# A decoder step on one core: the order of bias tables, row sums, gates and loads at its beginning rearranged

## The chip, the cores and the metric

One core of a Trainium2 chip runs the whole kernel. The engines named below are TensorE (PE, with its weight loads as PEld), VectorE (DVE), ScalarE (ACT), GpSimd (POOL) and SyncE (SP). SP and POOL issue nearly all DMAs. The metric is the device time of one execution in microseconds (us), as the median of several runs.

## What is computed

One layer of a decoder for 512 prompt tokens and 8 sample tokens (520 columns in all). The parts that the change touches are the conditioned norm, the projection, the branch gates, the compressed pages and the bias of the three attention branches:

```python
sh1, sc1, gt1, sh2, sc2, gt2 = ada_mod(c, ada_w, ada_b)       # silu(c) @ ada_w + ada_b
h = rmsnorm(x, norm1_g) * (1.0 + sc1) + sh1
xr, yg, q, kv_c, kv_s, kv_w, gl = split_columns(h @ w_in)
g = jax.nn.sigmoid(gl)                                         # three gates per head
...
# compressed branch of a sample: every page of the past, by page_table
past_c = cache_cmp[layer, page_table]
ck, ends = compress(chunk_proj(past_c, w1), w1, w2, pos)       # gelu, then w2
...
bias = rel_bias[t5_bucket(dist)]                               # 32 buckets x 8 heads
s = einsum('bqgrd,bkgd->bgrqk', q, k) * SCALE + bias
o_att = g[:, :, 0] * o_c + g[:, :, 1] * o_s + g[:, :, 2] * o_w
x = x + gt1 * (concat(rmsnorm(o_lru), rmsnorm(o_att)) @ w_out)
x = x + gt2 * PEER(h2)                                         # two thirds of the time
```

## The kernel before

Tokens lie along the free dimension, features on the 128 partitions. Each engine runs one program in its written order, and semaphores tie them together.

**Conditioning.** `ada_w` comes in four head groups of 2 MB (`load_head`, into three slots) and 32 tail tiles of 512 KB (`load_tail`). TensorE multiplies a group by `silu(c)` in `ada_step`, as eight products of 512 columns in four 32-row strips. ACT copies the result (`copy_m9`), TensorE turns it with four small products (`turn_m9`), and DVE adds the table (`shift_m`). All four head groups are needed before `h` exists.

**Front of TensorE.** Group 0, then, after all of `tables_loaded` (96, the last of the six loads being `rbx`, `rel_bias` repeated 16 times), `offset_bias(0)`, then the sum of squares of `x` as 16 products with `ones` (`two(0, ...)`), then groups 1 to 3, each with `turn_m9` and a piece of `offset_bias`. `offset_bias` makes the bias table of the compressed prompt branch (`pbias`) with 55 products of eight columns. Two further products at L628 and L629 make the bias rows `rsb`. DVE builds the root (`normed`, 520 columns wide), multiplies `x`, and applies scale and shift for eight feature chunks (`shifted`, L1332, one `h_ready` count each). Then come the gate columns (L640, 16 products with 24 output rows, a sigmoid on ACT, five transposes) and the projection loop `n = 0..17` (line L540, 16 products of 260 columns for each `n`). For `n >= 2` each `n` also carries two tail groups.

**Pages.** 64 pages of 128 KB fill `xpool`. SP issues pages 0 to 15 before it enters the loop over `n` and pages 16 to 31 in its step `n = 2`, ahead of the weight load for `n = 3`. POOL issues pages 32 to 63 once `ada_ready` is 3. Each issue reads the page number first (`page_rows`, L277 and L278). `hidden_pages(0)`, which stands in step `n = 4` of TensorE (L592), waits for all 64.

**Bias rows.** `rsb` goes to DRAM (`rscratch`) and is spread to 128 rows there (`rrows`). The 2 MB tile `biasT` of the prompt attention is loaded from it by POOL (L491) after `sel_free`. SP issues `wout` (4 MB), `xT` (2 MB) and nine copies of the window cache (4 MB) at the same signal.

**Sample attention.** `strips` (L713, L715) makes the logits of three branches. The third needs `kwin` and the one-hot table `ohw`, which SP loads after the last projection. Later come `hidden_prompt(1)` and `hidden_prompt(0)` (L701), with `hid` and bank 7 and 6 shared by the two, transposes (L757 to L763), and `outputs` (L780). Prompt attention adds `biasT` at L1537 on DVE.

## Time and profile before

| | us |
|---|---|
| median of 3 runs | 1961.47 (1959.98 to 1966.07) |
| the profiled execution, its own time | 1964.24 |
| its span, first to last instruction | 1962.6 |
| first projection product (n = 0) starts | 93.55 |
| first page product (L592) starts | 144.60 |
| last projection chunk done, sample attention starts | about 310 |
| `biasT` lands, prompt attention goes on | about 407 |
| output projection (L873) starts | 516.7 |
| mean granted TensorE clock | 0.947 |

TensorE is busy for 92% of the span. Up to 600 us the mean hides several stages with limits of their own. After that the two PEER loops keep TensorE close to full. The clock column is a share of full speed: 1.00 is 2.4 GHz, 0.50 is 1.2 GHz.

### The profile page before, as it was taken

What the parts mean: (1) busy time and instruction counts of PE and PEld (TensorE: products, weight loads), DVE (VectorE), ACT (ScalarE), POOL (GpSimd) and SP (SyncE); (2) the same over time, 40 slices, a digit from 0 to 9 for tenths busy, and PEclk for the clock granted to TensorE, in tenths of its full rate; (3) what the DMA queues carried; (4) which work ended last, traced back from release to release, by engine and by line L of the source; (5) the groups of instructions that cost most, each with busy time, mean ns of one, the idle gap of its engine ahead of it and who ended that gap; (6) DMA issues with size and microseconds to landing.
All of it is one profiled execution on the core that took longest, in us unless ns stands there. A gap on an engine that the chain in (4) does not pass through costs nothing.

```text
span 1962.6 us, 30207 instructions
## 1 busy us (share of the span) xinstructions
PE 1802.6 (92%) x11322; PEld 1670.6 (85%) x11322; DVE 1327.0 (68%) x2967; ACT 647.5 (33%) x1012; POOL 337.4 (17%) x362
## 2 busy tenths in 40 slices
PE   3889998757797999899999999999999999999996
PEld 2667785634586999899999999999999999999995
DVE  0310343347427778999999999995777777777775
ACT  1111332137313222333434334333333333333331
POOL 0301000000000000111123333432222222222220
PEclk9689998659998999999999999999999999999998
DMA  6573665230005322687679999998999999999981
GB/s 229 159 276 100 208 219 168 117 142 1 1 26 190 102 86 75 234 266 245 224 234 352 358 355 346 341 340 325 398 393 334 335 342 340 339 339 338 332 277 44
DMA packets 177773, 467.60 MB, mean 238 GB/s; under 512 B 20601, under 2 KB 91641, under 8 KB 175988
## 3 DMA queue, kind: packets, MB, share of 16 engines
q1 hardware_dynamic: 132788, 291.91, 42.8%
q0 software_dynamic: 44864, 174.14, 24.8%
q8 instruction: 68, 1.11, 0.2%
q14 instruction: 53, 0.43, 0.1%
HBM read 408.65 MB, written 64.14 MB: 241 GB/s over the span
## 4 chain that ended last, share of the span: by engine, by line
PE 83%; DVE 9%; DMA 4%; issue 2%; ACT 2%; SPq 0%; DVEq 0%; ACTq 0%; POOLq 0%
PE ps L1027 28%; PE ps L924 24%; PE ps L540 7%; PE ps L911 5%; PE ps L1008 4%; PE ps L873 3%; DMA arena<-rrows 1%; PE ps L592 1%; ACT arena L1061 1%; PE ps L563 1%; PE ps L849 1%; PE ps L549 1%; DMA cst<-in_rel_bias 1%; PE ps L841 1%; PE ps L898 1%
## 5 line engine op out<-in xcount | busy, mean ns | idle before, releaser
L1643 DVE TENSOR_TENSOR ul<-raw,uh 128x1024 fp32r<-128x1024 f32 x256 | 313.6, 1230 | 135.7 <-ACT uh L1061 117.5
L924 PE MATMUL ps<-hh,uh 128*128 128x392 f32 x1024 | 358.8, 350 | 5.8 <-DVE ul L1643 5.8
L1027 PE MATMUL ps<-ah,uh 128*128 128x392 f32 x1024 | 348.8, 341 | 2.7 <-DVE al L1848 2.7
L1027 PE MATMUL ps<-ah,ul 128*128 128x392 f32 x1024 | 350.9, 343 | 0.0
L1027 PE MATMUL ps<-al,uh 128*128 128x392 f32 x1024 | 350.2, 342 | 0.0
L924 PE MATMUL ps<-hl,uh 128*128 128x392 f32 x1024 | 350.0, 342 | 0.0
L924 PE MATMUL ps<-hh,ul 128*128 128x392 f32 x1024 | 349.0, 341 | 0.0
L1061 ACT ACTIVATE uh<-raw 128x1024 fp32r<-128x1024 f32 x256 | 270.3, 1056 | 116.4 <-PE ps L1027 106.1
L502 POOL DMA_INDIRECT xT<-in_u,gidx x128 | 148.2, 1158 | 591.1 <-DVE zg L1686 365.6
L502 POOL DMA_INDIRECT xT<-in_v,gidx x128 | 132.9, 1039 | 419.0 <-DVE vacc L1838 386.0
L924 PEld LDWEIGHTS ps<-hh,uh 128*128 128x128 f32 x1024 | 193.5, 189 | 8.7 <-DVE ul L1643 7.1
L1061 ACT ACTIVATE zbuf<-ps 128x392 f32<-128x392 f32 x128 | 63.8, 499 | 403.4 <-PE ps L924 349.8
L1027 PEld LDWEIGHTS ps<-ah,uh 128*128 128x128 f32 x1024 | 193.3, 189 | 3.0 <-issue 3.0
L924 PEld LDWEIGHTS ps<-hl,uh 128*128 128x128 f32 x1024 | 193.6, 189 | 0.0
L924 PEld LDWEIGHTS ps<-hh,ul 128*128 128x128 f32 x1024 | 193.4, 189 | 0.0
L1027 PEld LDWEIGHTS ps<-al,uh 128*128 128x128 f32 x1024 | 193.1, 189 | 0.0
L1027 PEld LDWEIGHTS ps<-ah,ul 128*128 128x128 f32 x1024 | 193.0, 189 | 0.0
L1838 DVE SCALAR_TENSOR_TENSOR vacc<-xT,ag,vacc 128x1024 f32<-128x1024 f32 x127 | 162.5, 1279 | 0.0
L1686 DVE CUSTOM_DVE_ANT_0 xT<-xT,hg 128x1024 f32<-128x1024 f32 x128 | 158.6, 1241 | 4.6 <-DMA xT<-in_u,gidx 4.6
L540 PE MATMUL ps<-arena 128*128 128x260 f32 x608 | 143.6, 395 | 16.2 <-issue 9.0
L540 PEld LDWEIGHTS ps<-arena 128*128 128x128 f32 x608 | 117.4, 196 | 36.6 <-issue 12.5
L1061 ACT ACTIVATE ah<-zin 128x392 fp32r<-128x392 f32 x128 | 68.3, 533 | 227.3 <-DVE zin L1845 227.3
(326 smaller groups left out, 2270.8 us busy)
## 6 DMA issues: line engine op xcount, KB each, us to landing
raw<-in_uT SPq DMA_DIRECT2D x128, 512.0 KB
raw<-in_v SPq DMA_DIRECT2D x128, 512.0 KB
zs<-zbuf SPq DMA_DIRECT2D x128, 196.0 KB
gw<-stage POOLq DMA_DIRECT2D x28, 896.0 KB
gr<-gw SPq DMA_DIRECT2D x32, 784.0 KB, 9.0
zin<-zs SPq DMA_DIRECT2D x128, 196.0 KB
arena<-in_ada_w SPq DMA_DIRECT2D x32, 512.0 KB, 4.6
arena<-in_w_in SPq DMA_DIRECT2D x18, 512.0 KB, 4.4
```

Of the source, the lines that this page charges most:

```text
L502: pool.indirect_dma_start(out=gb[:, s, :], out_offset=None, in_=table, in_offset=bass.IndirectOffsetOnAxis(ap=gidx[:, n:n + 1], axis=0)).t ...
L540: last = mm(ps[:, b + h, 0:HALF], lhs(k), rhs_k(k)[:, h * HALF:(h + 1) * HALF], start=(n == 0), stop=(n == len(ks) - 1))
L549: last = mm(ps[:, 2, m * NH:(m + 1) * NH], oha[0:33, st:st + P], rb[0:33], start=True, stop=True)
L873: last = mm(ps[:, 2 + 2 * (c % 3) + h, 0:HALF], wout[:, k, c * P:(c + 1) * P], zT[:, k, h * HALF:(h + 1) * HALF], start=(k == 0), stop=(k ...
L911: last = mm(ps[:, b + h, 0:HALF], weights[w](k), moving[m](k)[:, h * HALF:(h + 1) * HALF], start=(first and n == 0 and w == 0 and m == 0), ...
L924: last = mm(ps[:, bank, 0:DN], w[x][:, k * P:(k + 1) * P], m[:, k, G0:TOK], start=(k == 0 and x == 0 and m is hh), stop=(k == KD - 1 and x ...
L1008: last = mm(ps[:, 4 + n % 4, t * P:(t + 1) * P], oh[:, n % 6, t * P:(t + 1) * P], oh[:, n % 6, (4 + t) * P:(5 + t) * P], start=True, stop= ...
L1027: last = mm(ps[:, dc, 0:DN], w[:, q, cols], m[:, q, :], start=(first and w is uh and m is ah), stop=(final and w is ul))
L1061: return act.activation(out, in_, f, **kw)
L1643: tt(ul[:, i % 4, :], raw[:, i % 4, :], uh[:, i % 4, :].bitcast(F32), SUB).then_inc(S["lo_done"], 1)
L1686: dve.tensor_tensor_reduce(gb[:, n % 4, :], gb[:, n % 4, :], hg[:, :], 1.0, 0.0, MUL, ADD, zg[:, n:n + 1]).then_inc(S["ttr_done"], 1)
L1838: stt(vacc[:, :], gb[:, n % 4, :], ag[:, n:n + 1], vacc[:, :], MUL, ADD).then_inc(S["acc_step"], 1)
```

## The change

- Row sums. The sum of squares is made in four strips of 136 columns (`strip_sums`), the root on 136 columns (`inverse_strips`), and the result is spread back to 128 partitions in PSUM by five products (`spread_roots`). It now stands behind head group 1, and the root is ready ahead of group 3.
- Bias table `pbias`. The 55 products are gone. Eight products make a table `tofs`. POOL stores it to DRAM in eight pieces (`obias`) and reads `pbias` back in eight.
- `rbx` is no longer loaded. DVE copies it from `rb`. `tables_loaded` is waited for at 80.
- Gates. They are made behind projection chunk 0, in four strips, summed behind chunk 1 with `pick`, and the sigmoid comes last.
- The products of chunk 0 wait for one feature chunk each.
- Loads. The weights of chunks 0 and 1 go ahead of the pages. SP issues 12 pages before its loop, 4 in step 2 and 4 in step 3 behind the weights. POOL issues 44, from `ada_ready` 4 on. `w1p` goes behind the first 12 pages. `ohw` gets a place of its own and is loaded in step 5.
- `wout`, `xT` and what follows them on SP wait for `bias_loaded`.
- `hidden_prompt(0)` follows `hidden_prompt(1)` directly, with banks 1 and 0 and columns of `hid` of its own. The small products at L794 and after wait for `gelu_ready` 4.

```diff
             load(rb[0:32], io["rel_bias"], S["tables_loaded"])
+            load_head(1, 1)
             load(oha[0:33], io["oha"], S["tables_loaded"])
-            load_head(1, 1)
...
-            load(rbx[0:32].rearrange("p (b h) -> p b h", h=NH),
-                 io["rel_bias"].rearrange("a (o h) -> a o h", o=1).to_broadcast([32, P // NH, NH]), S["tables_loaded"])
             load(wgate, io["w_gate"], S["wgate_loaded"])
+            sp.wait_ge(S["ada_ready"], 3)
+            for n in range(2):
+                load(win_w[:, n * KD:(n + 1) * KD, :], io["w_in"][n], w_l[n])
...
-            load_pages(0, 16)
+            load_pages(0, 12)
+            load(w1p, io["w1p"], S["w1k_loaded"])
...
-                    load_pages(16, 32)
+                    load_pages(12, 16)
+                if n == 3:
+                    load_pages(16, 20)
+                if n == 5:
+                    load(ohw[0:33], io["ohw"], S["ohw_loaded"])
...
             sp.wait_ge(S["sel_free"], 1)
+            sp.wait_ge(S["bias_loaded"], 16)
             load(wout, io["w_out"], S["wout_loaded"])
...
+            pool.wait_ge(S["act_init"], 3)
+            pool.dma_start(rscratch, rsb[0:NH]).then_inc(S["scratch_stored"], 16)
             pool.wait_ge(S["page_loaded"], 16)
-            pool.wait_ge(S["ada_ready"], 3)
-            for n in range(32, 64):
+            pool.wait_ge(S["ada_ready"], ADA_HEAD)
+            for n in range(20, 64):
                 page_rows(pool, xpool[:, n, :], io["pool_c"], n, S["pages_k"])
...
+            def strip_sums(b, x, k, n):
+                for j in range(4):
+                    last = mm(ps[32 * j:32 * j + 32, b, 0:SW], ones[:, 0:32], x[:, k, j * P:j * P + SW],
+                              start=(k == 0), stop=(k == n - 1))
...
+                if g == 2:
+                    pe.wait_ge(S["act_init"], 2)
+                    for k in range(KD):
+                        last = strip_sums(0, hT, k, KD)
+                    last.then_inc(S["sum_ready"], 1)
+                    pe.wait_ge(S["tables_loaded"], 80)
...
+                if g == 3:
+                    pe.wait_ge(S["rstd_ready"], 1)
+                    spread_roots(1, 0)
...
-            hidden_prompt(1, 128)
+            hidden_prompt(1, 7, 128)
+            pe.wait_ge(S["w1k_loaded"], 48)
+            hidden_prompt(0, 1, 160)
...
+            link(tt(hT[:, :, 0:SEQ], xT[:, :, 0:SEQ], ps[:, 1:2, 0:SEQ].to_broadcast([P, KD, SEQ]), MUL),
```

How the program order moves at three places. TensorE from its first product to the first projection chunk, before (`ps` is PSUM, `arena` the big SBUF tile, the last field is the output shape with its count):

```order
L563 MATMUL ps<-arena 32x512 x8
L549 MATMUL ps<-cst,arena 128x8 x14
L540 MATMUL ps<-arena,ones 128x260 x16
L563 MATMUL ps<-arena 32x512 x8
L573 MATMUL ps<-arena 128x9 x4
L549 MATMUL ps<-cst,arena 128x8 x14
L563 MATMUL ps<-arena 32x512 x8
```

The same stretch of TensorE now:

```order
L581 MATMUL ps<-arena 32x512 x8
L591 MATMUL ps<-arena 128x9 x4
L561 MATMUL ps<-arena,ones 32x136 x32
L643 MATMUL ps<-arena,cst 8x512
L644 MATMUL ps<-arena,cst 8x128
L646 MATMUL ps<-cst,arena 128x8 x8
L581 MATMUL ps<-arena 32x512 x8
L591 MATMUL ps<-arena 128x9 x4
L568 MATMUL ps<-arena,ident 128x128 x4
L569 MATMUL ps<-arena,ident 128x8
```

The first rows of the new piece are head group 1 and its turn. The sums moved behind them, and the long rows of eight-column products shrank to eight.

SP between the gate weights and its first page, before:

```order
L284 DMA arena<-in_w_gate 128x192
L284 DMA cst<-in_newmask 128x8
L284 DMA cst<-in_gsum 128x128
L284 DMA cst<-in_validq 128x1
L284 DMA cst<-in_blkno 128x14
L284 DMA arena<-in_w_in 128x1024 x2
L284 DMA arena<-in_w1p 128x2048
L284 DMA arena<-in_posp 128x32
L284 DMA arena<-in_cmp_w 64x64 x4
```

And now:

```order
L288 DMA arena<-in_w_gate 128x256
L288 DMA arena<-in_w_in 128x1024 x2
L288 DMA cst<-in_newmask 128x8
L288 DMA cst<-in_gsum 128x128
L288 DMA cst<-in_validq 128x1
L288 DMA cst<-in_blkno 128x14
L288 DMA arena<-in_cmp_w 64x64 x4
```

The projection weights moved up and `w1p` left this place for one behind the pages.

TensorE in the sample attention, from the first prompt compression to the outputs, before:

```order
L701 MATMUL ps<-arena 64x31 x64
L757 MATMUL ps<-ident,arena 128x64 x4
L758 MATMUL ps<-ident,arena 8x64
L760 MATMUL ps<-ident,arena 63x64
L761 MATMUL ps<-ident,arena 8x64
L763 MATMUL ps<-ident,arena 128x64 x8
L767 MATMUL ps<-arena 31x128
L701 MATMUL ps<-arena 64x31 x64
L771 MATMUL ps<-arena 128x31
L780 MATMUL ps<-arena 32x128 x40
```

And now:

```order
L733 MATMUL ps<-arena 64x31 x128
L790 MATMUL ps<-ident,arena 128x64 x4
L791 MATMUL ps<-ident,arena 8x64
L794 MATMUL ps<-ident,arena 63x64
L795 MATMUL ps<-ident,arena 8x64
L797 MATMUL ps<-ident,arena 128x64 x8
L800 MATMUL ps<-arena 31x128
L801 MATMUL ps<-arena 128x31
L810 MATMUL ps<-arena 32x128 x40
```

The second block of 64 products moved ahead of the transposes.

## Rows read from the trace of the kernel before

**Rows 1.** The chain that ended last, 0 to 200 us: start, us, what

```profile
77.98 1.82 PE ps L573 x8
...
93.55 7.21 PE ps L540 x32
...
116.38 9.04 issue
125.42 8.96 PE ps L540 x32
...
144.60 13.96 PE ps L592 x128
```

**Rows 2.** DMA issues at 4.6 us: count, KB each, us to landing

```profile
arena<-in_ada_w SPq DMA_DIRECT2D x1, 2048.0 KB, 17.9
```

**Rows 3.** Timeline, 0 to 105 us: start, us, engine, line, shapes, idle before

```profile
14.67 0.60 ACT L1061 ACTIVATE arena<-ps 128x512 f32<-128x512 f32 x1 [11.28 <-PE ps L563]
...
34.01 6.14 PE L549 MATMUL ps<-cst,arena 33*128 33x8 f32 x28 [19.40 <-DMA cst<-in_rel_bias]
...
48.99 1.92 PE L563 MATMUL ps<-arena 128*32 128x512 f32 x16
...
56.15 3.64 PE L563 MATMUL ps<-arena 128*32 128x512 f32 x16
...
56.96 4.49 DVE L1324 TENSOR_TENSOR arena<-xT,arena 128x4160 f32<-128x4160 f32 x1 [0.70 <-ACT arena L1061]
...
81.07 3.74 DVE L1332 TENSOR_SCALAR arena<-arena,mT 128x512 f32<-128x512 f32 x8
```

**Rows 4.** Timeline, page issues of POOL and SP up to 121 us

```profile
76.05 0.56 POOL L278 DMA_DIRECT2D arena<-in_pool_c  x1 [1.00 <-issue]
...
102.99 0.54 POOL L278 DMA_DIRECT2D arena<-in_pool_c  x1 [0.64 <-issue]
...
102.83 18.16 SPq L278 DMA_DIRECT2D arena<-in_pool_c  x16
```

**Rows 5.** DMA issues, 0 to 110 us, with landings

```profile
arena<-in_pool_c POOLq DMA_DIRECT2D x32, 128.0 KB, 2.7
...
rrows<-rscratch POOLq DMA_DIRECT2D x1, 2560.0 KB, 13.6
```

**Rows 6.** Page loads as one tile: landing

```profile
DMA to landing us min/median/max: 2.0/3.1/13.0
```

**Rows 7.** Windows: PE, PEld, DVE, ACT, POOL busy, PEclk, DMA share, GB/s

```profile
65.00:70.00 5.00, 5.00 (x25) 3.17 (x29) 0.00 (x0) 0.00 (x0) 2.54 (x5) 0.50 1.02 344
```

**Rows 8.** Timeline, sample attention, 319 to 359 us

```profile
322.71 0.37 SPq L284 DMA_DIRECT2D arena<-in_ohw  x1
...
324.69 3.64 PE L713 MATMUL ps<-xT,arena 128*32 128x512 f32 x16 [5.29 <-issue]
...
335.74 3.93 PE L701 MATMUL ps<-arena 64*64 64x31 f32 x128
335.92 0.88 DVE L1488 MEMSET arena<- 128x984 f32 x1 [4.16 <-PE ps L540]
...
345.13 0.48 PE L760 MATMUL ps<-ident,arena 128*63 128x64 f32 x2 [4.22 <-DVEq L1518]
...
350.01 7.04 PE L701 MATMUL ps<-arena 64*64 64x31 f32 x128
...
358.38 4.96 PE L780 MATMUL ps<-arena 8*32 8x128 f32 x80
```

**Rows 9.** Chain that ended last, 200 to 520 us: the load of the bias tile

```profile
377.83 29.15 DMA arena<-rrows
```

**Rows 10.** Timeline of DVE from 383.5 us: its first use

```profile
407.00 0.29 DVE L1537 CUSTOM_DVE_ANT_0 arena<-ps,arena 128x128 f32<-128x128 f32 x1 [20.23 <-DMA arena<-rrows]
```

**Rows 11.** DMA queues, 370 to 420 us: packets, MB, share of 16 engines

```profile
q1 hardware_dynamic: 1584, 10.51, 54.0%
q0 software_dynamic: 528, 2.10, 10.3%
```

More of the change, by code:

```diff
@@ L176, in build @@
         w2 = at(42587, 2, P)
-        pbias = at(42843, NH, QM)
+        pbias = at(42843, QM, NH)
         rstd = at(43835, TOK)
-        wgate = at(44355, KD, 24)
+        roots = rstd[:, 0:SW]
+        wgate = at(43283, KD, 32)
+        tofs = at(43539, KD * NH)
         stc = at(44547, 4, 3 * NB)
@@ L198, in build @@
         sw = at(14552, 520)
-        ohw = at(15072, OHW_W)
+        ohw = at(43835, OHW_W)
         sc = at(45699, 64)
@@ L308, in _ @@
             load(blkno[:, 0:NSELB], io["blkno"], S["small_loaded"])
-            sp.wait_ge(S["ada_ready"], 3)
-            for n in range(2):
-                load(win_w[:, n * KD:(n + 1) * KD, :], io["w_in"][n], w_l[n])
-            load(w1p, io["w1p"], S["w1k_loaded"])
-            load(posp, io["posp"], S["pos_loaded"])
             sp.wait_ge(S["prep_done"], 1)
@@ L368, in _ @@
             sp.wait_ge(S["z_ready"], ZC)
-            load(ohw[0:33], io["ohw"], S["ohw_loaded"])
             load(vwin, io["win_v"].rearrange("b (c p) f -> p (b c) f", p=P), S["win_loaded"])
@@ L479, in _ @@
                            ).then_inc(S["rows_stored"], 16)
+            pool.wait_ge(S["scratch_stored"], 16 * 9)
+            for a in range(8):
+                pool.dma_start(pbias[16 * a:16 * a + 16], bass.AP(ob.tensor, (7 - a) * NH, [[64 * NH, 16], [NH, QM], [1, NH]])
+                               ).then_inc(S["rows_stored"], 16)
             pool.wait_ge(S["hid_ready"], 2)
@@ L662, in _ @@
                     pe.wait_ge(S["ri_ready"], n - 7)
-                two(2 * (n % 2), lambda k: win_w[:, (n % 2) * KD + k, :], lambda k: hT[:, k, :],
-                    range(KD)).then_inc(S["z_ready"], 1)
-                if n == 0:
-                    pe.wait_ge(S["gates_ready"], 1)
-                    for t in range(5):
-                        m = P if t < 4 else NB
-                        last = pe.transpose(ps[0:m, 7, 320 + t * 24:344 + t * 24], gT[0:24, t * P:t * P + m], ident[0:24, 0:24])
-                    last.then_inc(S["zg_ready"], 1)
+                for k in range(KD):
+                    if n == 0:
+                        pe.wait_ge(S["h_ready"], k + 1)
+                    for h in range(2):
+                        last = mm(ps[:, 2 * (n % 2) + h, 0:HALF], win_w[:, (n % 2) * KD + k, :],
+                                  hT[:, k, h * HALF:(h + 1) * HALF], start=(k == 0), stop=(k == KD - 1))
+                last.then_inc(S["z_ready"], 1)
+                if n == 0:
+                    gate_strips()
+                if n == 1:
+                    gate_sums()
                 if 7 <= n <= 13 and n % 2:
@@ L1053, in _, with link @@
             steps = [0]
-            def link(ins):
-                steps[0] += 1
-                ins.then_inc(S["act_step"], 1)
+            def link(*group):
+                for ins in group:
+                    steps[0] += 1
+                    ins.then_inc(S["act_step"], 1)
                 act.wait_ge(S["act_step"], steps[0])
@@ L1337, in shift_m @@
                    par[:, ADB + c0:ADB + c0 + n].to_broadcast([P, n, 9]), ADD).then_inc(S["mt_done"], 1)
-            dve.wait_ge(S["tables_loaded"], 96)
+            dve.wait_ge(S["tables_loaded"], 80)
+            link(cp(rbx[0:33].rearrange("p (b h) -> p b h", h=NH),
+                    rb[0:33].rearrange("p (o h) -> p o h", o=1).to_broadcast([33, P // NH, NH])))
             shift_m(0)
-            normed(hT, 1, 1, 0)
-            for i in range(1, ADA_HEAD):
-                shift_m(i)
+            shift_m(1)
+            dve.wait_ge(S["sum_ready"], 1)
+            inverse_strips(D, 0)
+            dve.wait_ge(S["roots_ready"], 1)
+            link(tt(hT[:, :, 0:SEQ], xT[:, :, 0:SEQ], ps[:, 1:2, 0:SEQ].to_broadcast([P, KD, SEQ]), MUL),
+                 tt(hT[:, :, SEQ:TOK], xT[:, :, SEQ:TOK], ps[:, 0:1, 256:256 + NB].to_broadcast([P, KD, NB]), MUL))
+            shift_m(2)
+            shift_m(3)
             dve.wait_ge(S["mt_done"], ADA_HEAD)
@@ L1562, in _ @@
             dve.wait_ge(S["pc_s"], 1)
+            dve.wait_ge(S["rows_stored"], 16 * 9)
             link(*[tt(pcb[:, i * NH:(i + 1) * NH, :].rearrange("p (g r) n -> p g r n", g=2),
                       ps[:, 2:4, i * GRP * NCMP_P:(i + 1) * GRP * NCMP_P].rearrange("p g (r n) -> p g r n", n=NCMP_P),
-                      pbias[:, :, 24 - 8 * i:24 - 8 * i + NCMP_P].rearrange("p (g r) n -> p g r n", g=2), ADD) for i in range(4)])
+                      pbias[:, 24 - 8 * i:24 - 8 * i + NCMP_P, :].rearrange("p n (g r) -> p g r n", g=2), ADD) for i in range(4)])
             link(dve.tensor_reduce(pcm[:, 0, :], pcb, AX.X, MAX))
```

145 lines of the change are left out of this document (73 added, 72 removed).

## The prediction, on record before the changed kernel ran

> **What bounds the kernel now.** I read the chain that ended last first, then the timeline of the beginning, the waits of TensorE, and the DMA issues with their landings. From 600 us on the two PEER loops keep TensorE full and the change does not touch them, so all is decided before 410 us. There four places matter.
>
> First, the beginning. TensorE does head group 0 and then idles 19.4 us for the last table, the repeated `rel_bias`, until 34.0 [rows 3]. That load queued behind head groups 2 and 3. Head group 1 had landed at 4.6 + 17.9 = 22.5 [rows 2]. From 34.0 to 81.1 TensorE works off what could have been done earlier, and the first projection chunk starts at 93.55, the first page product at 144.60 [rows 1]. Second, chunk 3 waits 9.04 us for its weights [rows 1], since SP spent 18.16 us on issuing 16 pages ahead of them [rows 4]. Third, the third strip of the sample attention waits 5.29 us, and what it waits for is the load of `ohw`, issued at 322.71 [rows 8]. Fourth, the bias tile takes 29.15 us to land, issued at 377.83 [rows 9], while DVE waits 20.23 us for it [rows 10].
>
> **Front, up to the first page product.** Most products here ran at 1.2 GHz: a head group took 3.64 us in one place and 1.92 in another [rows 3], and the granted clock is 0.50 in the window that I show [rows 7]. I work each step out at 2.4 and at 1.2 GHz. Head group: 1.9 or 3.6. Turn: 0.9 or 1.82 [rows 1]. ACT copy: 0.6 [rows 3]. Strip sums: 32 x 136 = 4352 columns in four strips against 8 x 512 = 4096 of a head group, so 2.0 or 3.9. The bias rows have 640 columns at 7.21/16 = 0.45 us per 260 [rows 1], so 1.1 or 2.2. The eight table products are 14 products in 6.14 us scaled [rows 3], 3.5 at 1.2 GHz and half of it at 2.4. The spread has 520 columns, 0.9 or 1.8.
>
> From 22.5: group 1, copy, turn, sums, bias rows and table end at 30.8 (fast) or 38.1 (slow). Group 2, copy, turn and spread end at 35.1 or 45.9. Group 3 ends at 37.0 or 49.5, and that is `ada_ready` 4. DVE multiplies `x` in 4.49 us [rows 3] from the end of the spread, to 39.6 or 50.4. The last copy and turn end at 38.5 or 51.9. Then 81.07 - 79.80 = 1.3 us of short DVE work [rows 1, 3] and one chunk of scale and shift, 3.74/8 = 0.5. Chunk 0 starts at 41.3 or 53.7. The small products and idle times between the groups make 1.2 GHz the commoner level there, so I go 0.6 of the way to the slow end: `ada_ready` 4 at 44.5, chunk 0 at 48.7.
>
> What is late next? POOL starts its pages at `ada_ready` 4. It spent (102.99 - 76.05)/23 = 1.17 us on each [rows 4], so 44 take 51. Landing of the last is 2.7 us in the median of its queue [rows 5] and up to 13.0 in the worst case of any page [rows 6]. I take 4, since the weights, `kwin` and tail tiles run beside it. The pages are complete at 44.5 + 51 + 4 = 99.5. TensorE itself would be there at 48.7 + 9.0 (chunk 0, as the one after an idle time [rows 1]) + 1.9 (gate strips, 4160 columns) + 7.2 + 0.5 + 8.2 + 8.7 + 8.7 = 92.9, each later chunk being 7.2 with 1.0 for the tail groups and 0.5 for turns. So the pages end last, and a new idle time of 6 to 7 us appears ahead of L592. After such a gap a chunk took 8.96 against 7.21 [rows 1], so 1.8 us more. The front gains 144.6 - 99.5 - 1.8 = **43.3 us**. The old wait of 9.04 us at chunk 3 is inside this sum: only 4 pages now stand between the weights, 4.5 us of SP time, under the 8 us of a chunk. Bounds: all fast with a landing of 2.7 gives 90.7 and a gain of 52. All slow with a landing of 13 gives 113.5 and a gain of 29.
>
> Covered and priced at nothing: the 16 small `obias` and `pbias` DMAs of POOL. They end by about 97 + 17 x 1.2 plus two landings, some 122, and POOL is next wanted when the page products end at about 133, while `pbias` itself is first read near 370 in the old time. Without that cover each would cost 1.2 us. The gate sums and the sigmoid lie beside chunk 2, the `rbx` copy beside the wait for group 1.
>
> The DMA traffic deserves a check. From 39 to 97 us pages, `w1p`, six weight chunks, six tail tiles and `kwin` make some 18 MB. At the 344 GB/s of the full window [rows 7] this is 52 us of 58. The Trainium skill, "DMA: Bandwidth & Descriptors", "Issuing engines are not separate DMA queues", says that issuing from several engines saves only the sequencer's time, since all run on the same 16 engines. By it the split would gain only the issue time and any shortage of bandwidth would stay. That is a rival below.
>
> **ohw.** With `ohw` there, TensorE goes on at 319.4 in the old time, at 2.4 GHz instead of 1.2: strip 1.9, one-hot part 1.0, and the sum of eight products 3.6, ending at 325.9. DVE then starts L1488 at 326.0 instead of 335.92 [rows 8]. The gain is **9.9 us**. If the clock is low anyway, only the wait of 5.29 goes.
>
> **hidden_prompt.** Before, the first block ran from 335.74, and TensorE reached `outputs` at 358.38, 22.6 us later, with a wait of 4.22 for DVE and 7.04 for the second block [rows 8]. Now the second block fills that wait. DVE still releases L760 after 9.4 us, but ACT needs its table load and two more Gelu pairs, 1.4 us, so 10.8. What follows is 13.25 - 7.04 - 0.8 = 5.4, in all 16.2, a gain of 6.4. If the second block takes 7.04 again, 12.9 + 5.4 = 18.3 and the gain is 4.3. I take **5.3**.
>
> **Bias tile.** Before, 2.10 MB of it shared 16 engines with 10.51 MB of SP's loads: its own packets took 10.3% of 50 us, 5.2 us of all engines [rows 11]. Alone it needs that and the smallest landing of any page, 2.0 us [rows 6], so about 7.2, and lands at 385.0. DVE is ready for it at 407.0 - 20.2 = 386.8 [rows 10]. The upper bound is the landing of `rrows`, 13.6 us in traffic [rows 5], which makes 391.4 and leaves 15.6. I take the lower one, since the queue is then empty, so the whole wait goes: **20.2 us**. What SP now issues later, `wout` and `xT`, is wanted at L873, more than 70 us after the new landing, and took 14 to 20 us before, so it costs nothing.
>
> The Trainium skill, "DMA: Bandwidth & Descriptors", "Anatomy of one DMA — SWDGE (gpsimd) path", fits a POOL-issued DMA as 2.0 us and bytes over 436 GB/s. For this tile it gives 6.8 us, and the sum would stay as it is. By the 13.6 us of the upper row it would be 4.6 us less.
>
> **The sum.** 43.3 + 9.9 + 5.3 + 20.2 = 78.7. The profiled execution took 1964.24, which becomes 1885.5. It was 2.8 us above the median of the runs shown, so I forecast 1961.5 - 78.7 = 1882.8, rounded 1883. All lower bounds, 29.3 + 5.3 + 4.3 + 15.6 = 54.5, give 1907. All upper ones, 52.1 + 9.9 + 6.4 + 20.2 = 88.6, give 1873.
>
> **Rivals.**
> (A) The pages are short of bandwidth, by the rule on shared engines above. `kwin` (2 MB), a weight chunk and two tail tiles fall into the last 12 us of the page issues: 5 MB with the pages in it, 14.5 us at 344 GB/s [rows 7]. If the last page then lands after the worst 13.0 us [rows 6] and not after 4, the time is 1892. For it: a DMA share of 1.02 at 65 to 70 us with pages in flight [rows 7]. Against it: only 52 of 58 us are filled. Chance 0.13.
> (B) The bias tile is slow of itself, because POOL must write its many short pieces, and not because of SP's loads. Then 5 us at most go and the time is 1898. For it: nothing but the 13.6 us of `rrows`. Against it: its packets fill only 5.2 us. Chance 0.09.
> (C) TensorE's clock is up through the beginning and the front ends near 91: 1875. Against it is the level of 0.50 while it did such work before. Chance 0.08.
> (D) Slower than before. POOL's pages now stand alone on the path, 44 in a row. If an issue cost more than 1.17 us, because reading the page number waits behind loads in full traffic, the front would pay 44 times that. The other gains are 35.4, so from 144.6 + 35.4 - 1.8 = 178 on, the kernel is slower, which is (178 - 48.5)/44 = 2.9 us a page. At 3.2 us the time is about 1973. Against it: the issues kept their pace at the full window too [rows 4, 7]. Chance 0.02.
> (E) The change does not do what it says, because some wait undoes the new order, as chunk 0 held back by its weights or by SP's first pages. Gains of the later three stay, 1926. Chance 0.02.
>
> **How the numbers follow.** My forecast has 0.66, with 1873 to 1907 as its own range. A, B and C lie inside or at its edge. I give 1868 to 1905, which leaves out D, E and the worst joint bounds, in all some 0.15. A measurement of this kernel tells 0.3%, about 6 us, from no change. Faster by more than that: 0.97. Within: 0.01. Slower: 0.02.
>
> **What would show it.** In the new profile: no idle time of TensorE for `rel_bias`. Chunk 0 starts between 41 and 54. POOL's 44 issues take 50 to 52 us from the end of group 3. The wait ahead of the first page product is 3 to 10 us and ends with a page, the first page product starts near 100. No wait over 2 us for the weights of chunk 3. Strip 3 follows at once on the small products. The bias tile lands within 9 us and DVE's wait for it is under 2. L873 starts near 438. It would be wrong if a page issue takes over 1.3 us, if the bias tile takes over 12 us, or if new waits for weights appear in chunks 5 to 17.

## The result, and the profile after

| | before, us | after, us |
|---|---|---|
| median (4 runs each) | 1960.72 (1958.52 to 1966.07) | 1883.72 (1879.04 to 1893.12) |
| the profiled execution, its own time | 1964.24 | 1879.04 |
| its span | 1962.6 | 1877.4 |
| mean granted TensorE clock | 0.947 | 0.965 |

The ratio is 0.9609, with a 95% interval from 0.9568 to 0.9651. The forecast was 1883, with 1868 to 1905. The profiled execution of after is the fastest of its four, so the two profiles differ by 85.2 us where the medians differ by 77.0. Busy time by engine on the page after:

```profile
PE 1759.1 (94%) x11275; PEld 1636.9 (87%) x11275; DVE 1324.3 (71%) x2967; ACT 646.8 (34%) x1013; POOL 368.4 (20%) x390
```

**The front.** Timeline of TensorE, DVE and POOL, 0 to 105 us: start, us, engine, line, shapes, count, and in brackets the idle time before with what ended it.

```profile
21.61 3.64 PE L581 MATMUL ps<-arena 128*32 128x512 f32 x16 [4.58 <-DMA arena<-in_ada_w]
26.96 2.06 PE L561 MATMUL ps<-arena,ones 128*32 128x136 f32 x64
...
30.12 1.95 PE L646 MATMUL ps<-cst,arena 33*128 33x8 f32 x16
44.81 0.58 POOL L282 DMA_DIRECT2D arena<-in_pool_c  x1 [10.83 <-issue]
46.95 8.66 PE L696 MATMUL ps<-arena 128*128 128x260 f32 x32 [1.98 <-DVE arena L1366]
...
66.19 7.28 PE L696 MATMUL ps<-arena 128*128 128x260 f32 x32 [0.53 <-DMA arena<-in_w_in]
...
74.41 7.28 PE L696 MATMUL ps<-arena 128*128 128x260 f32 x32
...
103.00 7.34 PE L610 MATMUL ps<-arena 128*64 128x256 f32 x44 [11.09 <-DMA arena<-in_pool_c]
```

The 19.40 us for the repeated `rel_bias` [rows 3] are gone. TensorE takes head group 1 when it lands and then works almost without a break. Its products lie at both clock levels: a head group took 3.64 us, and the strip sums of about the same length 2.06. Chunk 0 starts at 46.95 instead of 93.55 [rows 1]. Chunk 3 (74.41) has no wait, where it had 9.04 [rows 1]. Chunk 2 (66.19) has a small new one, 0.53 for its weights. In place of the old ones stands a new wait of 11.09 us ahead of the page products, and it ends with a page. The chain that ended last shows which one:

```profile
95.29 7.47 DMA arena<-in_pool_c
103.00 16.38 PE ps L610 x128
```

POOL's first page issue is at 44.81, its 44th at 95.29, so 1.174 us apart. The last one then took 7.47 us to land.

**Sample attention.** Timeline, 277 to 335 us:

```profile
277.27 1.92 PE L745 MATMUL ps<-xT,arena 128*32 128x512 f32 x16
...
280.12 3.77 PE L553 MATMUL ps<-arena,ones 128*128 128x260 f32 x16
283.99 4.39 PE L733 MATMUL ps<-arena 64*64 64x31 f32 x143
284.17 0.88 DVE L1526 MEMSET arena<- 128x984 f32 x1 [0.88 <-PE ps L553]
289.31 3.87 PE L733 MATMUL ps<-arena 64*64 64x31 f32 x113 [0.93 <-issue]
...
300.78 4.96 PE L810 MATMUL ps<-arena 8*32 8x128 f32 x80
```

The third strip (L745) has no wait and takes 1.92 us, not 3.64 after 5.29 [rows 8]. The second prompt block runs behind the first, with 0.93 idle between the pieces. The wait of 4.22 of TensorE [rows 8] is gone, and that of DVE has shrunk from 4.16 [rows 8] to 0.88.

**Bias tile.** The piece of the chain that ended last, and DVE's timeline:

```profile
319.39 9.08 DMA arena<-rrows
```

```profile
328.50 0.29 DVE L1575 CUSTOM_DVE_ANT_0 arena<-ps,arena 128x128 f32<-128x128 f32 x1 [0.92 <-DMA arena<-rrows]
```

It lands in 9.1 us, not 29.15 [rows 9], and DVE waits 0.92 for it, not 20.23 [rows 10].

Where the 85.2 us of the profiles went, by starts in the two timelines (the page products before start at 144.53 there, at 144.60 in the chain):

| stretch | before | after | gain | forecast |
|---|---|---|---|---|
| start to first page product | 144.5 | 103.0 | 41.5 | 43.3 with the next row |
| page products to first turn of the sample attention | 165.9 | 165.4 | 0.5 | |
| that turn to the issue of the bias tile | 67.4 | 51.0 | 16.4 | 15.2 |
| issue to first use of the bias tile | 29.2 | 9.1 | 20.1 | 20.2 |
| first use to output projection | 109.7 | 105.8 | 3.9 | 0 |
| output projection to the end | 1445.9 | 1443.1 | 2.8 | 0 |

### The profile page after: what moved, and what is told of

Read it like the earlier page. It is cut to its first block, busy times and chain, and to the rows that moved or that the text cites. A ratio compares the mean times of both kernels' runs of the same rounds, so it can differ in the third digit from the quotient of the medians.

```text
span 1877.4 us, 30131 instructions
## 1 busy us (share of the span) xinstructions
PE 1759.1 (94%) x11275; PEld 1636.9 (87%) x11275; DVE 1324.3 (71%) x2967; ACT 646.8 (34%) x1013; POOL 368.4 (20%) x390
## 4 chain that ended last, share of the span: by engine, by line
PE 82%; DVE 8%; DMA 3%; issue 2%; ACT 2%; POOLq 1%; SPq 1%; POOL 0%; DVEq 0%; ACTq 0%
PE ps L1057 29%; PE ps L954 25%; PE ps L941 5%; PE ps L1038 5%; PE ps L696 4%; PE ps L903 3%; PE ps L610 2%; ACT arena L1092 2%; PE ps L581 1%; PE ps L879 1%; DMA arena<-in_ada_w 1%; DMA arena<-in_w_in 1%; PE ps L928 1%; DVE arena L1575 1%; PE ps L810 1%
## 5 line engine op out<-in xcount | busy, mean ns | idle before, releaser
L1057 PE MATMUL ps<-ah,ul 128*128 128x392 f32 x1024 | 349.8, 342 | 0.0
L515 POOL DMA_INDIRECT xT<-in_u,gidx x128 | 163.5, 1278 | 576.0 <-DVE zg L1725 342.7
L696 PE MATMUL ps<-arena 128*128 128x260 f32 x576 | 133.6, 391 | 8.6 <-DMA arena<-in_w_in 5.2
L696 PEld LDWEIGHTS ps<-arena 128*128 128x128 f32 x576 | 110.2, 194 | 26.8 <-DMA arena<-in_w_in 5.5
```

The lines of the kernel that those rows point to most:

```text
L515: pool.indirect_dma_start(out=gb[:, s, :], out_offset=None, in_=table, in_offset=bass.IndirectOffsetOnAxis(ap=gidx[:, n:n + 1], axis=0)).t ...
L696: last = mm(ps[:, 2 * (n % 2) + h, 0:HALF], win_w[:, (n % 2) * KD + k, :], hT[:, k, h * HALF:(h + 1) * HALF], start=(k == 0), stop=(k == K ...
L1057: last = mm(ps[:, dc, 0:DN], w[:, q, cols], m[:, q, :], start=(first and w is uh and m is ah), stop=(final and w is ul))
```

## Experiments

**1. The wait for `bias_loaded` taken out.** SP again issues its loads beside the tile.

```diff
             sp.wait_ge(S["sel_free"], 1)
-            sp.wait_ge(S["bias_loaded"], 16)
             load(wout, io["w_out"], S["wout_loaded"])
```

> The changed kernel with the wait of SP for the bias tile taken out, nothing else. Theory (the loads of wout, xT and the window copies slowed the tile): it lands 25 to 30 us after its issue again instead of 9.1, DVE waits about 20 us, the time rises by 20 us to about 1904. Rival (the tile was slow for another reason that the new front removed, such as PE or POOL order): it lands in 9 to 14 us here too and the time rises by under 5 us.

Measured: 1901.99 us, ratio 0.9713 (0.9668 to 0.9757), so 18.3 us above the changed kernel. Timeline of DVE, then the DMA view, 321 to 355 us, with the tile in flight from 322.0 to 349.8 (queues with packets, MB, share of 16 engines, then the issue with KB and us to landing):

```profile
349.87 0.29 DVE L1574 CUSTOM_DVE_ANT_0 arena<-ps,arena 128x128 f32<-128x128 f32 x1 [18.29 <-DMA arena<-rrows]
```

```profile
q1 hardware_dynamic: 1561, 10.48, 80.1%
q0 software_dynamic: 528, 2.10, 15.1%
...
arena<-rrows POOLq DMA_DIRECT2D x1, 2048.0 KB, 27.8
```

The tile takes 15% of the engines' time in this window, the other queue 80%, and the landing is 27.8 us. Rival B, a tile that is slow of itself, falls: with SP's loads held back the same tile landed in 8.7 to 10.1 us in all eleven kernels that have the wait.

**2. The same wait alone, in the kernel before.**

```diff
             sp.wait_ge(S["sel_free"], 1)
+            sp.wait_ge(S["bias_loaded"], 16)
             load(wout, io["w_out"], S["wout_loaded"])
```

> The kernel before with this alone: SP waits for the bias tile ahead of wout and xT. Theory: the tile lands 9 us after its issue, DVE's wait falls from 20 us to under 1, time about 1941. Rival (it needs the quiet of the other edits): gain under 10 us.

Measured: 1939.99 us, ratio 0.9894 (0.9879 to 0.9908), a gain of 20.7. The chain and DVE's timeline:

```profile
377.12 10.10 DMA arena<-rrows
```

```profile
387.24 0.29 DVE L1538 CUSTOM_DVE_ANT_0 arena<-ps,arena 128x128 f32<-128x128 f32 x1 [1.33 <-DMA arena<-rrows]
```

One line brings the whole 20 us with nothing else changed, and the same line taken out of the changed kernel loses 18. The term stands from both sides, and nothing that SP now issues later is missed.

**3. `ohw` loaded where it was before,** behind the last projection.

```diff
-                if n == 5:
-                    load(ohw[0:33], io["ohw"], S["ohw_loaded"])
...
+            load(ohw[0:33], io["ohw"], S["ohw_loaded"])
```

> The changed kernel with the ohw load put back behind the last projection chunk. Theory (the table's load was what the third strip waited for): TensorE idles about 5.3 us ahead of the strip, the strip then runs at 1.2 GHz, and the start of the DVE work behind the sums is 9 to 10 us later, time about 1893. Rival (the low clock there has its own cause): only the idle time of 5.3 us comes back, 1889.

Measured: 1891.49 us, ratio 0.9653 (0.9608 to 0.9698), so 7.8 above the changed kernel, with four times from 1881.78 to 1899.11. Timeline, 276 to 300 us:

```profile
281.91 3.48 PE L744 MATMUL ps<-xT,arena 128*32 128x512 f32 x16 [4.33 <-issue]
286.31 3.77 PE L552 MATMUL ps<-arena,ones 128*128 128x260 f32 x16
...
290.36 0.88 DVE L1525 MEMSET arena<- 128x984 f32 x1 [2.42 <-PE ps L552]
```

The wait of 4.33 and the slower strip (3.48, not 1.92) are back, together 5.9 us on the way from the turn to DVE's start at the memset (21.7 against 15.8). But the sum of eight products behind it stays at 3.77, where it took 5.51 before, and the hidden blocks run in one piece of 7.66, without their gap of 0.93, so the way to `outputs` is only 4.3 longer (36.7 against 32.4). Undoing the load alone costs 4.3 to 5.9 by the trace. From before to after the stretch to the memset lost 9.7. Most of the rest is the clock of the products behind the wait. The strip ran at the low level in both (granted clock 0.50 before, 0.54 here). Before, the one-hot part stayed at 0.50 and the sum had 0.67. Here both had 1.00. The trace is nearer to the rival (only the wait) than to the theory, and the median lies between them.

The kernel before is the exception here. In experiments 2 and 10, which keep its old order at this place, the wait was 4.97 and 4.60 us and the sum behind it took 3.77 in both:

```profile
326.56 3.52 PE L714 MATMUL ps<-xT,arena 128*32 128x512 f32 x16 [4.97 <-issue]
...
331.01 3.77 PE L541 MATMUL ps<-arena,ones 128*128 128x260 f32 x16
```

That is from experiment 2. From the turn to the memset it is 25.5 us before, 22.4 and 22.1 in experiments 2 and 10, 21.7 here, and 15.8 in all ten kernels with the early load. So the load is worth 5.9 to 6.6 us there in three of four comparisons, and 9.7 only against the profiled execution of before.

**4. The second prompt block where it was before,** with its Gelu pair and its old banks.

```diff
-            pe.wait_ge(S["w1k_loaded"], 48)
-            hidden_prompt(0, 1, 160)
...
-            pe.wait_ge(S["gelu_ready"], 4)
...
+            pe.wait_ge(S["gelu_ready"], 3)
...
+            pe.wait_ge(S["w1k_loaded"], 48)
+            hidden_prompt(0, 7, 160)
+            pe.wait_ge(S["gelu_ready"], 4)
```

> The changed kernel with hidden_prompt(0) back behind the small transposes, in the banks and columns of before. Theory (the second block filled a wait for DVE): outputs start 5 to 6 us later relative to the first block, time about 1889. Rival (the gain came from the clock, not from the filled wait): under 3 us, and the second block takes 3.9 us in its old place too.

Measured: 1886.87 us, ratio 0.9631 (0.9604 to 0.9659). TensorE, 279 to 309 us:

```profile
286.01 3.93 PE L733 MATMUL ps<-arena 64*64 64x31 f32 x128
...
295.39 0.47 PE L791 MATMUL ps<-ident,arena 128*63 128x64 f32 x2 [4.21 <-DVEq L1558]
...
300.28 7.04 PE L733 MATMUL ps<-arena 64*64 64x31 f32 x128
```

The old wait and the old length of the second block come back (4.21 and 7.04, as in [rows 8]), and from L733 to the outputs it is 22.6 us, against 16.8 with the change. The term is 5.8 for this pair of traces. The median moved by 3.2, which by itself is inside the scatter of both. Over all kernels the stretch is 22.6 in each of the four with the old order, but 15.1 to 20.1, 18.2 in the mean, in the ten with the new one. So the change is worth 2.5 to 7.5 us, 4.4 in the mean. In experiment 1, one of the slow ones (20.1), the idle time inside the second block was 1.90 us, and its last 113 products then ran at a granted clock of 0.50:

```profile
288.66 6.19 PE L732 MATMUL ps<-arena 64*64 64x31 f32 x113 [1.90 <-issue]
```

In the changed kernel the same piece took 3.87 after 0.93.

**5. The old split of the pages** (32 by SP, 32 by POOL), with the start at `ada_ready` 4 kept.

```diff
-            load_pages(0, 12)
+            load_pages(0, 16)
...
-                    load_pages(12, 16)
-                if n == 3:
-                    load_pages(16, 20)
+                    load_pages(16, 32)
...
-            for n in range(20, 64):
+            for n in range(32, 64):
...
-                    pe.wait_ge(S["gather_k"], 16 * 20)
-                    pe.wait_ge(S["pages_k"], 16 * 44)
+                    pe.wait_ge(S["gather_k"], 16 * 32)
+                    pe.wait_ge(S["pages_k"], 16 * 32)
```

> The changed kernel with 16 pages of SP ahead of its loop, 16 in step 2 and 32 on POOL, as before, POOL still starting at ada_ready 4. Theory (issue time of the pages sets the front, 1.15 us each on POOL and 0.9 to 1.1 on SP): POOL is done 14 us earlier, at about 81, but chunk 3 waits 7 to 9 us for its weights since 16 pages stand ahead of them. The first page product starts at 100 to 103, so the time is within 3 us of the changed kernel. Rival (the split is worth the 9 us wait that it removes): the first page product starts 8 to 10 us later than 103 and the time is about 1893.

Measured: 1889.27 us, ratio 0.964 (0.9613 to 0.9668). Timeline, 55 to 112 us:

```profile
65.46 17.24 SPq L282 DMA_DIRECT2D arena<-in_pool_c  x16
70.80 9.08 PE L694 MATMUL ps<-arena 128*128 128x260 f32 x32 [5.18 <-DMA arena<-in_w_in]
...
86.98 9.50 PE L694 MATMUL ps<-arena 128*128 128x260 f32 x32 [6.09 <-issue]
...
108.62 3.67 PE L608 MATMUL ps<-arena 128*64 128x256 f32 x32
```

POOL is done with its pages at 79.4 here, so nothing waits for POOL. TensorE itself is late: it lost 5.18 and 6.09 us to weights that stood behind SP's pages, and the chunks behind the two waits took 9.08 and 9.50 instead of 7.28. I had expected a tie within 3 us. The page products start 6.7 us later than the mean of 101.9 of four kernels with the changed front (below), and the median is 5.6 above the changed kernel. The new split is worth that, though it creates a wait of its own ahead of the page products (11.09 in the changed kernel, 5.9 to 6.6 in the other three of the four).

**6. POOL's pages start one group earlier,** at `ada_ready` 3. A change of one number on the changed kernel, which tells whether POOL's chain of issues sets the end of the front.

```diff
-            pool.wait_ge(S["ada_ready"], ADA_HEAD)
+            pool.wait_ge(S["ada_ready"], ADA_HEAD - 1)
```

> The changed kernel with POOL's pages released at ada_ready 3 instead of 4, 8.2 us earlier (35.0 against 43.25). Theory (44 issues of 1.15 us are what ends last): the first page product starts 7 to 8 us earlier, at about 95, time about 1876. Rival (the traffic of pages, kwin and weights ends last, whoever issues): the last landings do not move by more than 2 us, and the chunk weights land later, time 1882 to 1885.

Measured: 1879.86 us, ratio 0.9593 (0.9564 to 0.9622). Timeline, 37 to 98 us:

```profile
37.30 0.58 POOL L282 DMA_DIRECT2D arena<-in_pool_c  x1 [3.12 <-issue]
...
96.99 1.55 PE L610 MATMUL ps<-arena 128*64 128x256 f32 x6 [3.29 <-DMA arena<-in_pool_c]
```

Against the means of the four kernels with the changed front, the issues start 5.9 us earlier (37.30, mean 43.2) and the page products 4.9 earlier (96.99, mean 101.9). The other 1.0 is the landing, 8.99 against 8.0 in the mean. POOL's chain was the bound. With it 6 us earlier, the wait ahead of the page products is down to 3.29. Chunk 2 waits 2.30 for its weights, which is inside the 0.5 to 2.7 of the four.

**7. `kwin` (2 MB) four steps later,** to see whether it is what slows the last page.

```diff
-                if n == 4:
+                if n == 8:
                     sp.wait_ge(S["h_ready"], KD)
                     load(kwin, io["win_kT"], S["x_loaded"])
```

> The changed kernel with the 2 MB kwin load moved from step 4 to step 8 of SP's loop, behind the page products. Theory (the issues set the end, the landing is 2.7 us without heavy traffic beside it): the last page lands 2.5 to 4 us after its issue instead of 7.5, the first page product starts 4 to 5 us earlier, time about 1879. Rival (small obias stores or the w_in and tail tiles hold the last pages up): landing stays over 6 us, no gain.

Measured: 1882.33 us, ratio 0.962 (0.9587 to 0.9652). The chain, 85 to 101 us:

```profile
92.21 6.95 DMA arena<-in_pool_c
```

6.95 against 7.47, so taking `kwin` away is not enough, as the rival had it, and TensorE still waited 9.41 us. But it is not cleared by this. With `kwin` gone, the two `wlru` loads, in runs of 256 B, fell into the landing: they were issued at 89.92 and 91.34 and landed at 96.78 and 98.25, and of the 1384 packets that SP's queue moved from 92.21 to 99.16 us, 1101 were under 512 B.

**8. `kwin` and `wlru` both later.**

```diff
-                if n == 4:
+                if n == 8:
...
-                if n == 5:
+                if n == 7:
                     sp.wait_ge(S["prep_done"], 4)
```

> The changed kernel with kwin in step 8 and the two wlru loads (256-byte runs) in step 7 of SP's loop, both behind the page products. Theory (many short runs issued at 92 us sit on the engines ahead of the last pages): the last page lands 3 to 4 us after its issue instead of 7 to 9, and the first page product follows POOL's last issue by under 4.5 us. Rival (weights, tail tiles or POOL's own queue delay it): landing stays at 6 us and more.

Measured: 1883.6 us, ratio 0.9596 (0.9575 to 0.9618). Chain, and TensorE's timeline:

```profile
97.48 3.87 DMA arena<-in_pool_c
```

```profile
101.69 8.57 PE L610 MATMUL ps<-arena 128*64 128x256 f32 x62 [2.79 <-DMA arena<-in_pool_c]
```

The landing falls to 3.87 us, as the theory had it. With the loads of the changed kernel in place it was 7.3 to 9.1 in seven kernels (after, and experiments 1, 3, 4, 6, 9 and 11). But the small packets are not shown to be the reason. Only in the profile of after did they fall into the landing. In the other six `wlru` was issued behind the last page, and what was in flight was `kwin`, with weights and tail tiles. DMA view from the issue of the last page to its landing, SP's queue (packets, MB, share of 16 engines), in the order after (95.3 to 102.8 us), experiment 11 (85.8 to 94.9) and this one (97.5 to 101.4):

```profile
q1 hardware_dynamic: 1307, 1.52, 82.2%
q1 hardware_dynamic: 459, 3.27, 91.5%
q1 hardware_dynamic: 177, 0.65, 48.9%
```

The landings were 7.47, 9.05 and 3.87 us. Experiment 11, with the longest, had fewer packets under 512 B in both queues together (177) than any of the other six (285 to 1226). What goes with a long landing is the share that SP's queue takes: 70 to 92% in the seven and 75% in experiment 7, against 49% here and 36% in experiment 5, where POOL's last page took 3.4 us. So `kwin` and `wlru` together cost the last page 3 to 5 us, and one of them is enough to keep it near 7 us or above. What packet size adds was not tested apart.

The time did not follow, for two reasons. Chunk 0 happened to start at 50.3 in that execution, 4 us later than the mean of the four, and POOL with it, so the page products began at 101.69, where the mean is 101.9. And the moved loads were wanted: TensorE now waits for them behind the page products, and the stretch from there to the sample attention is 170.4 us, against 166.7 in the mean of the four.

```profile
165.91 1.53 PE L553 MATMUL ps<-arena 128*128 128x260 f32 x4 [2.18 <-DMA arena<-in_wlru]
```

**9. The repeated `rel_bias` loaded again,** in place of DVE's copy, with `tables_loaded` at 96.

```diff
+            load(rbx[0:32].rearrange("p (b h) -> p b h", h=NH),
+                 io["rel_bias"].rearrange("a (o h) -> a o h", o=1).to_broadcast([32, P // NH, NH]), S["tables_loaded"])
...
-                    pe.wait_ge(S["tables_loaded"], 80)
+                    pe.wait_ge(S["tables_loaded"], 96)
...
```

> The changed kernel with rbx loaded from DRAM again (behind head group 3) and the tables waited for at 96. Theory (order in the queue: this small load lands only with head group 3, at about 33.5): the bias rows wait from 29 to 33.5, everything behind slips 4 to 5 us, POOL's pages too, time about 1888. Rival (the wait of 19 us of before comes back whole): first chunk 19 us later, about 1902.

Measured: 1893.07 us, ratio 0.9681 (0.9647 to 0.9714). TensorE, 20 to 60 us:

```profile
34.36 1.87 PE L645 MATMUL ps<-arena,cst 33*8 33x512 f32 x2 [2.43 <-DMA cst<-in_rel_bias]
...
36.59 3.58 PE L648 MATMUL ps<-cst,arena 33*128 33x8 f32 x16
...
53.35 7.01 PE L698 MATMUL ps<-arena 128*128 128x260 f32 x21 [3.09 <-DVE arena L1368]
```

The wait is 2.43, since the changed kernel has other work for TensorE up to there. But the table products behind it ran at 1.2 GHz (3.58 for what took 1.95). Chunk 0 and the page products came 7.1 and 6.7 us later than the means, where 4 to 5 were expected, and the median is 9.4 above the changed kernel.

**10. DVE's copy of `rbx` alone, in the kernel before.**

```diff
-            load(rbx[0:32].rearrange("p (b h) -> p b h", h=NH),
-                 io["rel_bias"].rearrange("a (o h) -> a o h", o=1).to_broadcast([32, P // NH, NH]), S["tables_loaded"])
...
-                    pe.wait_ge(S["tables_loaded"], 96)
+                    pe.wait_ge(S["tables_loaded"], 80)
...
+            link(cp(rbx[0:33].rearrange("p (b h) -> p b h", h=NH),
+                    rb[0:33].rearrange("p (o h) -> p o h", o=1).to_broadcast([33, P // NH, NH])))
```

> The kernel before with this alone: rbx copied by DVE instead of loaded, tables waited for at 80. Theory (TensorE's own work fills the beginning from 34 on): the bias products start near 23 instead of 34, then head groups 1 to 3 land in time, and the first projection chunk starts 10 to 11 us earlier, time about 1950. Rival (POOL's and SP's pages or head group 3 take the place of the wait): gain under 5 us.

Measured: 1950.26 us, ratio 0.9954 (0.9938 to 0.9971), a gain of 10.5. TensorE:

```profile
23.06 6.14 PE L547 MATMUL ps<-cst,arena 33*128 33x8 f32 x28 [8.38 <-DMA arena<-in_ohd]
...
83.95 7.28 PE L538 MATMUL ps<-arena 128*128 128x260 f32 x32
```

The wait falls from 19.40 [rows 3] to 8.38, since the next table, `ohd`, still stands behind head group 1 in the queue, and chunk 0 gains 9.6. So of the 46.6 us by which chunk 0 moved, this one load carries about a fifth. The rest needs the sums, the table and the gates out of the way as well.

**11. POOL's pages two groups earlier,** at `ada_ready` 2.

```diff
-            pool.wait_ge(S["ada_ready"], ADA_HEAD)
+            pool.wait_ge(S["ada_ready"], ADA_HEAD - 2)
```

> The changed kernel with POOL's 44 pages released at ada_ready 2 (25.3 us) and nothing else. Theory (with the issues out of the way TensorE's own work sets the front): POOL is done near 77, the wait ahead of the first page product is gone and it starts at 90 to 93, against 99 to 105 in the runs so far, time about 1874. Rival (pages now take bandwidth from head group 3 and from the first weights): chunk 0 starts over 3 us later than 48 or chunk 2 waits over 3 us for weights, and the time stays at 1880 or above.

Measured: 1878.19 us, ratio 0.9575 (0.956 to 0.9589). POOL's first page, and the chain:

```profile
35.40 0.58 POOL L282 DMA_DIRECT2D arena<-in_pool_c  x1 [0.95 <-issue]
```

```profile
85.83 9.05 DMA arena<-in_pool_c
```

It began at 35.40 and not near 25, because ahead of it on POOL stands the store of the bias rows, which waits for `act_init` 3 and went out at 33.86. TensorE waits 1.72 only, and the page products are at 95.12, which is 6.8 ahead of the mean, between the theory (90 to 93) and the rival. This is the best version measured: 5.5 us under the median of the changed kernel. The two intervals overlap, so a gain over it is likely but not settled.

**12. All of it together:** `ada_ready` 3, SP takes 24 pages (four more in step 4), POOL 40, `kwin` and `wlru` later.

```diff
                 if n == 4:
+                    load_pages(20, 24)
+                if n == 8:
                     sp.wait_ge(S["h_ready"], KD)
                     load(kwin, io["win_kT"], S["x_loaded"])
-                if n == 5:
+                if n == 7:
...
-            pool.wait_ge(S["ada_ready"], ADA_HEAD)
-            for n in range(20, 64):
+            pool.wait_ge(S["ada_ready"], ADA_HEAD - 1)
+            for n in range(24, 64):
...
```

> The changed kernel with POOL released at ada_ready 3, 40 pages on POOL and 24 on SP (four more in step 4), and kwin and wlru behind the page products. Theory: POOL is done near 83, the last page lands by 88, the first page product starts at 90 to 92 with TensorE still at 2.4 GHz, time about 1873. Rival (traffic bound): first page product at 96 or later and 1880.

Measured: 1884.68 us, ratio 0.9605 (0.9574 to 0.9635), no gain. Its six times go from 1871.84 to 1893.88, and the profile is of one at 1890.74. Timeline, 45 to 106 us, and the landing of the last of SP's four pages in the DMA view:

```profile
88.00 3.67 SPq L282 DMA_DIRECT2D arena<-in_pool_c  x4
...
104.74 1.54 PE L612 MATMUL ps<-arena 128*64 128x256 f32 x6 [8.70 <-issue]
```

```profile
arena<-in_pool_c SPq DMA_DIRECT2D x1, 128.0 KB, 13.2
```

The last page is now SP's. SP reaches step 4 only when TensorE frees a weight buffer, so its four pages go out from 88.0 to 91.7, as late as POOL's 44th went out in experiment 7. The first two land in about 4 us, the last two in 11.5 and 13.2, beside POOL's bias-row traffic. TensorE waits 8.70 us, as the rival had it. POOL's own last page had landed at 87.8. Fewer pages on POOL helped nothing in this execution, since the end of the pages moved to the other queue. Behind the page products it again waits for `wlru` (2.37 us), and that stretch is 171.4 us.

## Why the prediction was right

**What bounds.** All four places were the right ones. Nothing of the gain comes from elsewhere but the last two rows of the table. Across all thirteen kernels and the one before, the stretch from the first use of the bias tile to the output projection is 105.3 to 109.8 us, and from there to the end it is either 1443.0 to 1443.3 (nine kernels) or 1445.8 to 1446.0 (five), whatever the edit. The profiled execution of before had the longer of both (109.7, 1445.9), the one of after the shorter (105.8, 1443.1). These 6.7 us are scatter that the profiled pair happened to have. The row of the sample attention (16.4, forecast 15.2) holds scatter too, in favour of the forecast. From the first turn to the issue of the bias tile it is 67.4, 64.5 and 64.2 us in the three kernels with both old orders (before, experiments 2 and 10), and 49.6 to 55.3 in the nine with both new ones, so 12.2 between the means. Without the 4.2 that the pair has over this, 85.2 - 6.7 - 4.2 = 74.3, beside a forecast sum of 78.7 and a difference of medians of 77.0. The places and the mechanisms were right and the sum is good to a few us. That single terms agree with one pair of profiles to 0.2 us is luck.

**Front, 43.3 forecast, 42.0 measured** (41.5 and 0.5). `ada_ready` 4 came at 43.3 (44.5 forecast), chunk 0 at 46.95 (48.7), POOL's 44 pages took 50.5 from first to last issue (51), TensorE was ready at 91.9 (92.9), and the first 128 page products took 16.4 instead of 14.0 at the clock behind the gap (1.8 forecast, 2.4 measured). The term that was mis-sized is the landing of the last page: 4 forecast, 7.47 measured, on a median of 2.7 [rows 5] where the worst case of 13.0 [rows 6] also stood. It goes with the traffic of SP's queue beside it (experiments 7 and 8), for which the forecast had allowed 1.3 us over that median. `ada_ready` 4 being 1.2 us earlier made up for a part. Less the slower first block, 39.1 us of the 41.5 were left there, but 1.7 came back at the chunk behind the page products (7.25 at 149.83, against 8.94 before) and some more in the chunks after it, which makes the 0.5 of the table. Four executions with this front (after, and experiments 1, 3 and 4) put the page products at 99.3 to 104.8, 101.9 in the mean, so the forecast of 99.5 is 2.4 early. The new wait was forecast at 6 to 7 and named as what is late next. It was 11.09 in the changed kernel and 5.9 to 6.6 in the other three, where chunk 2 waited 1.2 to 2.7 for its weights and then took 8.97 to 10.28 instead of 7.28, so that TensorE came later. Experiments 6 and 11 show that POOL's start sets when it ends.

**Bandwidth (rival A).** It was partly there. The engines are full while the pages end, and the last page took nearly twice what I gave it. The 344 GB/s that I took for a full window was not the most they move: from 83 to 92 us it was 382. Windows of the changed kernel, 83 to 92 and 96 to 103 us: PE, PEld, DVE, ACT, POOL busy, granted clock, DMA share, GB/s.

```profile
83.00:92.00 9.00, 8.91 (x71) 7.41 (x70) 3.21 (x18) 3.70 (x7) 4.04 (x9) 1.00 1.00 382
...
96.00:103.00 7.00, 0.00 (x1) 0.03 (x1) 0.00 (x0) 0.00 (x0) 4.59 (x9) 0.50 1.13 289
```

The Trainium skill, "DMA: Bandwidth & Descriptors", "Issuing engines are not separate DMA queues", says that splitting over engines saves only sequencer time. The trace agrees with its sense and shows the size of what it leaves: the split saved 6.7 us (experiment 5), which I read as SP's issue time ahead of the weights and the slower chunks behind those waits. The second row also shows the clock in the gap: 0.50 in its last 7 us, which hold no product. The first 128 page products behind it took 16.4 us and the next 128 took 14.0.

**ohw, 9.9 forecast, 9.7 measured.** The wait came as worked out (5.29). The agreement of the clock part is luck: the forecast read it from the one profile in which the clock stayed low behind the strip. In the three other kernels with the late load (experiments 2, 3 and 10) one-hot part and sum ran at 2.4 GHz, and the load is worth 5.9 to 6.6 there. What decides whether the clock comes back at once is open.

**hidden_prompt, 5.3 forecast, 5.85 measured,** and 5.8 by experiment 4, but 4.4 in the mean of all kernels (2.5 to 7.5). The forecast had 4.3 and 6.4 as its ends, by the clock of the second block. That is what differs between experiment 1 and the changed kernel, but the kernels spread more widely than the two ends. Behind it, one cost that I had at nothing: DVE's four additions of `pbias` take 2.14 us where they took 1.39. The table is now laid out the other way and read with a stride, which is the likely reason; no run has it alone. With it the way from `outputs` to the bias issue still gained 0.8.

```profile
309.65 2.14 DVE L1602 TENSOR_TENSOR arena<-ps,arena 128x248 f32<-128x248 f32 x4 [8.96 <-PE ps L833]
```

**Bias tile, 20.2 forecast, 20.1 measured.** The landing is 9.1 and not 7.2, but DVE was ready 8.2 us after the issue, not 8.9, so the wait that stays is 0.92. Experiments 1 and 2 give 18.3 and 20.7. The Trainium skill, "DMA: Bandwidth & Descriptors", "Anatomy of one DMA — SWDGE (gpsimd) path", gives an estimate of 6.8 us for this tile by its formula. The trace has 9.1 and 10.1 for the tile alone, and 27.8 and 29.2 beside SP's loads, which the formula does not speak of.

**The other rivals.** C did not come: the front stood between the two levels, with a gap ahead of the page products. D fell, as POOL kept 1.17 us an issue. E fell, as chunk 0 waited for DVE and not for weights. Chunk 2 has a new wait for weights, 0.53 here and 1.2 to 2.7 in experiments 1, 3 and 4. The one of 3.88 us at 172.9 was there before as well, with 4.19.

## What to carry to other kernels

A load that nobody seems to wait for long can hold up one that is on the path, because they share the engines: look at what else is issued at the same signal, and let the large, late-wanted loads wait for the small, early-wanted one (20 us here for one line). When a wait is removed, forecast the next-late thing as start of its queue + number of issues x time of one + landing, and take the landing from rows with the same traffic, not from the median of a quiet queue. Moving work from one queue to another only helps if the other reaches it in time, and the queue's own position in its program decides that (experiment 12). A load that is moved out of the way must still be there when it is wanted (experiments 8 and 12). And before a term is called measured, look for the same stretch in every kernel that shares it: two terms here moved by 3 to 5 us between kernels with the same order at that place.

## What the runs showed of the hardware that I had not expected

- The landing of POOL's last 128 KB page goes with what SP's queue has in flight beside it: 7.3 to 9.1 us in seven kernels where that queue took 70 to 92% of the engines' time, 3.9 and 3.4 us where it took 49 and 36% (experiments 8 and 5). Taking one of two loads away (experiment 7) changed little, 6.95 us at 75%.
- The same front ends at different times from execution to execution: chunk 0 at 44.6 to 50.3 us, with the clock level of the products ahead of it. An edit worth 3 us there can't be told from one profile.
- An idle time lowers the clock of what follows by differing lengths: behind 5.29 us of waiting [rows 8] the sum of products after the strip took 5.51 us, behind 4.33, 4.97 and 4.60 us in experiments 3, 2 and 10 it took 3.77.
- The last stretch of 1443 us has two values 2.8 us apart and nothing in between. What chooses is open. No run was made on it.
